# Modulation rows computed in two column halves, inside the feature projection and the preceding output projection

## The reference, cut to what matters

```python
def _layer(x, c, p):
    mod = jax.nn.silu(c) @ p['ada_w'] + p['ada_b']        # c: one row of 1024 per sequence, ada_w: 1024 x 3072
    shift, scale, gate = jnp.split(mod, 3, axis=-1)
    h = rms_norm(x, p['norm_w']) * (1 + scale[:, None, :]) + shift[:, None, :]
    z = h @ p['w_in']                                     # feature columns (1792) and token columns (1504)
    ...                                                   # RWKV-7 scan, latent attention, spatial gating
    y = jnp.concatenate([y_a, y_b, y_c], axis=-1) @ p['w_out']
    return x + gate[:, None, :] * y
```

## Time and profile before

| | |
|---|---|
| median of three runs | 5666.72 us |
| the profiled execution | 5676.56 us, its span 5674.8 us |
| TensorE busy | 5361.2 us, 94% |
| VectorE, ScalarE, GpSimd busy | 50%, 36%, 12% |
| layer 1: `modulation` | about 0 to 60 us |
| layer 1: `feature_projection` | about 60 to 582 us |
| layer 2: `modulation` | 2834 to 2893 us |
| layer 2: `feature_projection` | 2893 to about 3416 us |
| granted clock of TensorE over the span | 0.973 |

### The profile page before, as it was taken

The page is one execution under the profiler, slowest core; times in us unless marked ns, Lnnn a source line. Parts: engine busy times, 40 slices in busy tenths (PEclk is TensorE's granted clock), DMA queues, the critical chain, the costliest instruction groups (busy, mean ns, idle before and its releaser), DMA issues. The chain is left out here.

```text
span 5674.8 us, 101589 instructions
## 1 busy us (share of the span) xinstructions
PE 5361.2 (94%) x42636; PEld 2906.3 (51%) x42636; DVE 2855.3 (50%) x4296; ACT 2070.2 (36%) x3469; POOL 682.1 (12%) x1070
## 2 busy tenths in 40 slices
PE   7999999989989999989989999999899899999899
PEld 2444344477874444445434443444777744444454
DVE  1222376645545555556522223866455455555465
ACT  1121455344444444431111214553444444444311
POOL 0000000045430000001100000000444400000011
PEclk9999999999999999999989999999999999999999
DMA  6121565465542111025362215654655421110243
GB/s 247 70 91 54 182 205 188 150 157 139 140 111 64 24 24 41 11 89 177 120 239 80 80 58 179 206 186 150 156 139 136 111 68 24 24 38 15 88 173 122
DMA packets 648069, 646.54 MB, mean 114 GB/s; under 512 B 226937, under 2 KB 509049, under 8 KB 640381
## 3 DMA queue, kind: packets, MB, share of 16 engines
q1 hardware_dynamic: 647176, 638.89, 36.6%
q10 hardware_dynamic: 440, 1.15, 0.1%
HBM read 372.80 MB, written 267.13 MB: 113 GB/s over the span
## 5 line engine op out<-in xcount | busy, mean ns | idle before, releaser
L434 PE MATMUL ps<-feat_hT,w_features 128*128 128x512 f32 x2240 | 972.3, 592 | 0.0
L752 PE MATMUL ps<-w_tokens,prep_hT 128*128 128x512 f32 (+1 forms) x1920 | 825.9, 590 | 19.8 <-DMA prep_hT<-s_ht 19.8
L1629 PE MATMUL ps<-att_K,att_Q 96*128 96x512 f32 x1632 | 745.0, 599 | 33.4 <-DMA att_K<-s_qkt 23.8
L434 PEld LDWEIGHTS ps<-feat_hT,w_features 128*128 128x128 f32 x2240 | 420.5, 190 | 504.1 <-issue 501.5
L1743 DVE TENSOR_REDUCE att_mx<-ps 128x1 f32<-128x1024 f32 x384 | 470.3, 1225 | 286.5 <-PE ps L1629 286.5
L752 PEld LDWEIGHTS ps<-w_tokens,prep_hT 128*128 128x128 f32 x1920 | 365.2, 192 | 471.4 <-issue 449.1
L1636 PEld LDWEIGHTS ps<-kc,att_pr 128*128 128x128 f32 x3264 | 363.0, 141 | 432.8 <-issue 319.0
L2007 PE MATMUL ps<-w_out,fin_yT 128*128 128x512 f32 x1280 | 569.1, 598 | 2.5 <-DVE fin_yT L1965 2.5
L1636 PE MATMUL ps<-kc,att_pr 128*128 128x128 f32 x3264 | 478.9, 279 | 5.3 <-DVE att_PT L1752 2.5
L1707 ACT ACTIVATE att_PT<-ps 128x512 f32<-128x512 f32 x384 | 227.9, 594 | 691.7 <-PE ps L1636 691.7
L1629 PEld LDWEIGHTS ps<-att_K,att_Q 96*128 96x128 f32 x1632 | 297.1, 192 | 336.2 <-issue 257.2
(11 more groups left out here) (222 smaller groups left out, 7354.7 us busy)
## 6 DMA issues: line engine op xcount, KB each, us to landing
s_sc<-prep_sc SPq DMA_DIRECT2D x20, 3072.0 KB, 9.6
scan_src<-s_sc SPq DMA_DIRECT2D x80, 768.0 KB, 8.0
mod_ada<-in_ada_w SPq DMA_DIRECT2D x16, 1536.0 KB, 9.1
s_qkt<-scan_work SPq DMA_DIRECT2D x40, 576.0 KB, 4.7
fin_z<-s_zt SPq DMA_DIRECT2D x40, 576.0 KB, 5.2
s_zf<-feat_co SPq DMA_DIRECT2D x88, 256.0 KB, 2.5
s_ht<-feat_hT SPq DMA_DIRECT2D x10, 2048.0 KB, 7.8
prep_hT<-s_ht SPq DMA_DIRECT2D x40, 512.0 KB, 5.5
```

The source lines that it names most:

```text
L434: last = pe.matmul(b, wf[:, k, i * P:(i + 1) * P], hT[g % 2][:, k, :], start=(k == 0), stop=(k == KD - 1))
L752: last = pe.matmul(ps[:, tiles.bank(pieces[n]), 0:c1 - c0], hT[j % NH][:, k, :], wt[:, k, c0:c1], start=(k == 0), stop=(k == KD - 1))
L1629: pe.matmul(ps[:, c, :], Q[:, t * P:(t + 1) * P], K[:, k0:k0 + G], start=True, stop=True).then_inc(scored, 1)
```

## The change

The stage `modulation` is gone. Its work stands in two other places:

- Layer 1, in `feature_projection`: SyncE loads x(0) in four pieces, then shift and scale columns of `ada_w` in eight slices through five buffers laid over `w_tokens`, then `w_features` in five pieces, then the gate columns (4096 KB, over the same place). TensorE forms `h` 0 to 5, then the 32 products of shift and scale, the small transposes, then `h` 6 and 7.
- Layer 2, in `out_projection` of layer 1: the slices are loaded after tiles 0 to 7; the four products of a slice follow `p(n,0)` of tiles 9 to 16, the small transposes follow `p(17,0)`. Their sums stay in banks 6 and 7, so the list of banks has six.
- The gate rows of both layers: 16 products at the end of group 0 of `feature_projection`; `w_tokens` is loaded only after them.

A product of the modulation now has two column halves: the columns of one go to partitions 0 and 1 of a bank, those of the other to partitions 64 and 65. The sums of squares of group 0 wait piece by piece. The bias of shift and scale comes as columns, and `amod` has two entries and no longer five. `feature_projection` has 47 semaphores in place of 20, `out_projection` 42 in place of 30.

```diff
         kc = sb("kc", [P, K_ALL])
-        col = sb("col", [P, C_ALL])
-        amod = sb("amod", [P, NG, 2, KD])
+        cols = [sb(f"col{l}", [P, C_ALL]) for l in range(LAYERS)]
+        sg = sb("sg", [P, KD, 2])
+        amod = sb("amod", [P, 2, 2, KD])
         eps = sb("eps", [P, 4])
         ident = kc[:, K_ID:K_ID + P]
-        sems = dict(nc=nc, d=d, ps=ps, kc=kc, col=col, amod=amod, eps=eps, ident=ident)
+        sems = [dict(nc=nc, d=d, ps=ps, kc=kc, col=cols[l], amod=amod, eps=eps, ident=ident) for l in range(LAYERS)]
...
         for l in range(LAYERS):
             with nc.sbuf_tensor(f"w_tokens{l}", [P, KD, WT], F32) as wt:
                 with nc.sbuf_tensor(f"w_features{l}", [P, KD, WF], F32) as wf:
-                    modulation(l, wf, **sems)
-                    feature_projection(l, wf, wt, wt_in, **sems)
-                token_projection(l, wt, wt_in, **sems)
-            rwkv_scan(l, **sems)
...
+BANK_M = 6
+
+
+def modulation_products(pe, ps, ada, sg, k):
+
+    for b in range(2):
+        for c in range(2):
+            at = 512 * (2 * b + c)
+            last = pe.matmul(ps[64 * c:64 * c + 2, BANK_M + b, :], sg[:, k, :], ada[:, at:at + 512], start=(k == 0), stop=(k == KD - 1))
+    return last
+
+
+def modulation_turned(pe, ps, rows, ident):
+
+    for b in range(2):
+        for m in range(4):
+            for c in range(2):
+                half, at = slice(64 * c, 64 * c + 2), 2 * (4 * b + m)
+                last = pe.transpose(ps[:, BANK_M + c, at:at + 2], rows[half, 512 * b + m * P:512 * b + (m + 1) * P], ident[half, 64 * c:64 * c + 2])
+    return last
+
+
+def modulation_columns(v, ps, col, amod, summed):
+
+    made = ps[:, BANK_M:BANK_M + 2, 0:16].rearrange("p c (b m s) -> p b s c m", b=2, s=2)
+    column = lambda at: col[:, at:at + KD].rearrange("p (c m) -> p c m", c=2).unsqueeze(1).to_broadcast([P, 2, 2, 4])
+    scale, shift = (amod[:, :, n, :].rearrange("p s (c m) -> p s c m", c=2) for n in range(2))
+    v.tensor_tensor(scale, made[:, 1, :, :, :], column(C_ADAB + KD), ALU.add).then_inc(summed, 1)
+    v.wait_ge(summed, 1)
+    v.scalar_tensor_tensor(scale, scale, 1.0, column(C_NORM), ALU.add, ALU.mult).then_inc(summed, 1)
+    v.tensor_tensor(shift, made[:, 0, :, :, :], column(C_ADAB), ALU.add).then_inc(summed, 1)
+
...
+        if g == 0:
+            order.append(("gate", 0, 0))
     for u in order:
-        uses.add(u, "dve" if u[0] == "h" else "act")
+        uses.add(u, "act" if u[0] == "f" else "dve")
+
+    NA = 5
+    flat = wt[:, :, :].rearrange("p k n -> p (k n)")
+    ada = [flat[:, 2 * D * n:2 * D * (n + 1)] for n in range(NA)]
+    ada_g = flat[:, 0:KD * D].rearrange("p (k n) -> p k n", k=KD)
+    parts = [(0, 1), (1, 2), (2, 4), (4, 8), (8, NFB)]
...
-                block, x_in, zeroed, square_sums, roots, normed, filled, act_out, dve_out, edges, centre, tapped, conv, kept0, kept1, o0, o1, o2, o3, g0, g1):
+        ct = sb("ct", [P, KD, 2])
+        gb = sb("gb", [P, 512])
+        gr = sb("gr", [P, 512])
+        mrows = sb("mrows", [P, 2 * 512]) if l == 0 else None
...
                 def load_x(g):
                     if g:
                         sp.wait_ge(filled, uses.ready(("h", g - 1, KD - 1)))
-                    sp.dma_start(x[:, :, :], (d["x"] if l == 0 else d["xs"])[g * G:(g + 1) * G, :].rearrange("(j p) n -> p j n", p=P)).then_inc(x_in, 16)
+                        sp.dma_start(x[:, :, :], rows_of[g * G:(g + 1) * G, :].rearrange("(j p) n -> p j n", p=P)).then_inc(x_in, 16)
+                    else:
+                        for j in range(TPG):
+                            sp.dma_start(x[:, j, :], rows_of[j * P:(j + 1) * P, :]).then_inc(first[j], 16)
...
                 load_x(0)
-                sp.dma_start(wt[:, :, :], d["w_t"][:, l * KD:(l + 1) * KD, :]).then_inc(wt_in, 16)
+                if l == 0:
+                    for n in range(KD):
+                        if n >= NA:
+                            sp.wait_ge(used, n - NA + 1)
+                        sp.dma_start(ada[n % NA], d["ada_w"][:, n, 0:2 * D]).then_inc(part[n % NA], 16)
+                for n, (m0, m1) in enumerate(parts):
+                    sp.dma_start(wf[:, :, m0 * P:m1 * P], d["w_f"][:, l * KD:(l + 1) * KD, m0 * P:m1 * P]).then_inc(wf_in[n], 16)
+                if l == 0:
+                    sp.wait_ge(made, 1)
+                sp.dma_start(ada_g, d["ada_w"][:, l * KD:(l + 1) * KD, 2 * D:3 * D]).then_inc(ada_g_in, 16)
...
+                    if g == 0:
+                        sp.wait_ge(gate_s, 1)
+                        emptied(sp, ("gate", 0, 0))
+                        for c in range(2):
+                            sp.dma_start(d["gate"][:, 512 * c:512 * (c + 1)], gr[64 * c:64 * c + 2, :]).then_inc(gate_sent, 16)
+                        sp.wait_ge(filled, uses.ready(("gate", 0, 0)))
+                        sp.dma_start(wt[:, :, :], d["w_t"][:, l * KD:(l + 1) * KD, :]).then_inc(wt_in, 16)
+                sp.wait_ge(gate_sent, 32)
...
-                    a.wait_ge(x_in, 16 * (g + 1))
                     if g:
+                        a.wait_ge(x_in, 16 * g)
...
                     for j in range(TPG):
+                        if g == 0:
+                            a.wait_ge(first[j], 16)
...
+                if l == 0:
+                    a.dma_start(ct[:, :, :], d["c"]).then_inc(c_in, 16)
+                    for n in range(LAYERS):
+                        a.dma_start(cols[n][:, :], d["cols"][n * P:(n + 1) * P, :]).then_inc(c_in, 16)
+                    a.dma_start(kc[:, :], d["consts"]).then_inc(consts_in, 16)
+                for c in range(2):
+                    n0 = R_ADAB + 2 * D + 512 * c
+                    a.dma_start(gb[64 * c:64 * c + 2, :], d["rows"][l:l + 1, n0:n0 + 512].to_broadcast([2, 512])).then_inc(bias_in, 16)
+                if l == 0:
+                    a.wait_ge(c_in, 16 * (1 + LAYERS))
+                    a.activation(sg[:, :, :], ct[:, :, :], ACT.Silu).then_inc(silu, 1)
                 square(0)
+                if l == 0:
+                    a.wait_ge(made, 1)
+                    for b in range(2):
+                        a.activation(mrows[64:66, 512 * b:512 * (b + 1)], ps[64:66, BANK_M + b, :], ACT.Copy).then_inc(rows_s, 1)
...
+                if l == 0:
+                    v.memset(eps[:, 0:3], -0.5).then_inc(setd, 1)
+                    v.memset(eps[:, 3:4], 1.0).then_inc(setd, 1)
                 normalise(0)
+                if l == 0:
+                    v.wait_ge(c_in, 16 * (1 + LAYERS))
+                    v.wait_ge(made, 1)
+                    for b in range(2):
+                        v.tensor_copy(mrows[0:2, 512 * b:512 * (b + 1)], ps[0:2, BANK_M + b, :]).then_inc(rows_s, 1)
+                    v.wait_ge(turned, 1)
+                    modulation_columns(v, ps, col, amod, amod_s)
+                    v.wait_ge(amod_s, 3)
                 for k in range(KD):
...
+                    if g == 0:
+                        u = ("gate", 0, 0)
+                        v.wait_ge(bias_in, 32)
+                        v.wait_ge(filled, uses.ready(u))
+                        for c in range(2):
+                            rows = slice(64 * c, 64 * c + 2)
+                            v.tensor_tensor(gr[rows, :], ps[rows, uses.bank(u), :], gb[rows, :], ALU.add).then_inc(dve_out if c else gate_s, 1)
...
             @block.tensor
             def _(pe):
+                if l == 0:
+                    pe.wait_ge(consts_in, 16)
...
+                    if l == 0 and u == ("h", 0, BANK_M):
+                        pe.wait_ge(silu, 1)
+                        for n in range(KD):
+                            pe.wait_ge(part[n % NA], 16 * (n // NA + 1))
+                            last = modulation_products(pe, ps, ada[n % NA], sg, n)
+                            last.then_inc(made if n == KD - 1 else used, 1)
+                        pe.wait_ge(rows_s, 4)
+                        modulation_turned(pe, ps, mrows, ident).then_inc(turned, 1)
+                        pe.wait_ge(amod_s, 3)
...
+                    elif name == "gate":
+                        pe.wait_ge(ada_g_in, 16)
+                        for k in range(KD):
+                            for c in range(2):
+                                last = pe.matmul(b[64 * c:64 * c + 2, :], sg[:, k, :], ada_g[:, k, 512 * c:512 * (c + 1)], start=(k == 0), stop=(k == KD - 1))
                     else:
+                        for n, (m0, m1) in enumerate(parts):
+                            if g == 0 and i == m0:
+                                pe.wait_ge(wf_in[n], 16)
...
         if n + 1 < NT:
             order += [("sv", n + 1), ("ya", n + 1), ("yb", n + 1), ("yc", n + 1)]
         order += [("p", n, 1)]
-    uses = Uses()
+    uses = Uses(BANK_M)
...
+        more = l + 1 < LAYERS
+        ada = sb("ada", [P, KD, 2 * D]) if more else None
+        mrows = sb("mrows", [P, 2 * 512]) if more else None
+        FIRST = 9
...
@@ -1863,6 +1920,8 @@
```

(45 more changed lines are left out.)

26 lines of the change are left out of this document (18 added, 8 removed).

## The result

The changed kernel takes 5607.7 us (median of 4 runs, 5606.5 to 5608.5); the kernel before, beside it on the same chip, 5668.3 (5664.6 to 5676.9). The ratio is 0.9891, with an interval of 0.9874 to 0.9908: faster by 1.1%. The forecast was 5597.6, range 5584 to 5621.

What follows compares the result with a forecast made beforehand. TensorE, busy 94% of the span, was taken as the bound, with idle time at both layers' starts. Won 43.4 and 62.0, paid 36.3: 69.1 us off, taken from the runs' median, gives 5597.6 us, range 5584 to 5621.

Steps and rivals of the forecast that it cites:

- layer 1, first feature product: Start of layer 1: first feature product at 39.3 us instead of 82.7, 43.4 us won.
- x(1) of layer 1 lands: Layer 1's loads: x(1) lands at 70 to 72 us against a limit of 75, covered by 3 to 4 us.
- I take the difference off the median: Last step: the saving from an execution of 5676.6 us, 9.8 above the runs' median, is subtracted from that median, giving 5597.6.
- The sum: Whole kernel: 43.4 won in layer 1 plus 62.0 in layer 2, less 36.3 paid, gives 69.1 us off.
- the first three pieces are squared meanwhile: Layer 1's start: three pieces of x(0) are squared during loading, the last takes 1.2 us, done at 11.6.
- hidden, by 1 us: Layer 1's modulation products: the last slice lands at about 32 us, its products start at 33.2, so no wait.
- idle for 1 to 2 us: Layer 1's load queue: the sixth slice waits for a buffer until slice 0 is used (22.7), idling the queue 1 to 2 us.
- its limit: Feature stage: x(1) may land 35.7 us after the first feature product without delaying group 1; in layer 1, at 75 us.
- A: Rival: column halves do not overlap in long sequences of modulation products; saved 27.7 us, time 5639; chance 0.08.
- B: Rival: loads come late, with 1 to 2 us for a lower clock; +7, 5605, or 5616 at 0.30 MB/us; chance 0.14.
- C: Rival: six banks stall TensorE, 40 tiles taking 72 us and more; 5670 to 5690; chance 0.02.
- D: Rival: overlap starts earlier, semaphores cost nothing and x(0) lands sooner; 5588; chance 0.06.

Runs made afterwards that it cites:

- the other order: Changed kernel with a slice's four products issued as banks 0 and 1 of the first half, then of the second; 5610.3 us, ratio 0.9885.
- two slices first: Changed kernel with the products of slices 0 and 1 issued ahead of the first transposes of layer 1; 5603.5 us, ratio 0.9876.
- both improvements: Changed kernel with slices 0 and 1 multiplied before the first transposes and semaphores cleared by four engines; 5596.2 us, ratio 0.9874.
- the delay of 5.2 us: Changed kernel with 1920 KB more, unused, queued ahead of x(1) in both layers; x(1) landed 5.2 us later; 5616.3 us, ratio 0.9894.
- one column half: Changed kernel with the second column half of slices 1 to 6 written to the first's partitions, sums wrong; 5637.4 us, ratio 0.9935.

## Why the prediction was right, and what was off

The mechanism held, and most terms did. In us:

| step | foreseen | measured |
|---|---|---|
| layer 1, first feature product | 39.3 | 41.36 |
| layer 2, first feature product into the stage | 19.2 | 18.7 |
| gate rows of layer 1 | 7.1 | 7.0 (first instruction to the next of another kind) |
| a slice in the output projection | 1.96 | 2.02 |
| small transposes in the output projection | 1.4 and 0.3 | 1.5, of which 0.63 is the wait for VectorE |
| a semaphore | 0.06 | 0.063, of which 0.058 from one clear to the next |
| tile without a slice, six banks | no longer | 15.50, no longer |
| x(1) of layer 1 lands | 70 to 72 | 76.4 |
| x(1) of layer 2, after the issue of x(0) | 46 to 48 | 49.1 |

**The number** was 10.1 us too low, and the step that made most of this is the last one: "I take the difference off the median." The sum came from an execution of 5676.6 us, and 5676.6 less 69.1 is 5607.5; the changed kernel's profiled execution took 5607.75. By the profiled executions the step off the median made 9.9 us of the miss, and the sum 0.2.

That 0.2 is partly luck. The stages that the change touches (layer 1's start, output projection of layer 1 and features of layer 2, last output projection) take 1829.4 and 1828.8 us in the two profiles of the kernel before, 1761.6 and 1762.7 in those of the changed one: 66 to 68 less, so the sum was 1 to 3 too high, mostly by the start of layer 1. The other stages take 3845.4 and 3843.9 before, 3844.4 and 3845.6 after, and 3836 to 3852 in the versions that leave the semaphores alone: the scatter between executions lies there (the first token stage took 547.1 and 541.8 in two profiles of the same changed kernel).

The medians say less. On the two occasions on which both kernels ran beside each other they are 60.6 and 59.9 apart. On the two others the kernel before was slower (5676.1 and 5674.1), and on the first of these the other order, whose stages are those of the changed kernel but for a fall of the clock, was 65.8 below it. Both profiles of the kernel before are of executions of 5674 to 5677 us, so they don't show where the faster ones save time. The change is worth 60 us by the medians and 66 to 68 by the stages of the profiled executions; what the difference is stays open, and with it whether the median was a bad number to start from.

**Layer 1's start** came 2.1 us late. The prediction had "the first three pieces are squared meanwhile"; but the first sum of squares stands behind the Silu on ScalarE, and that waits for its columns until 7.97. So the four run in series and end at 12.95; the last piece has landed at 11.17, where the prediction had 10.4, so with one left to do they would have ended at 12.4. The transposes began at 17.33 and not 15.8: 0.8 us by the landing, 0.6 by the Silu, the rest in roots and scaling. The last slices cost 0.2 and 0.69 us of waiting, where I had put "hidden, by 1 us". The window 22.6 to 33 has 263 GB/s: the queue stands still, for slices 5 to 7 need buffers which only products at 22.6 and later set free. The fifth slice has landed at 24.01, the sixth is issued at 24.55 and lands at 29.36; the prediction had "idle for 1 to 2 us" here. The run with two slices first has no such wait. Its products end 4.6 us earlier, 3.4 of them by two slices that no longer stand behind the transposes and 0.9 by the waits, and the clock took back 0.6 before the first feature product. The run with both improvements has waits of 0.19 and 0.69 again, and its products end at the same time (33.10 and 33.14).

**x(1)** came 4 to 6 us later than foreseen in layer 1. About half of it has the same cause: what wasn't moved before 33 was still to be moved, and with two slices first, where the queue doesn't stand still, x(1) lands 3.3 us earlier (73.11). The other 1 to 3 us stay open. I had its limit right in kind: group 1 was ready 1.2 us before TensorE wanted it, where I foresaw 3 to 4, and the delay of 5.2 us produced a wait of 3.24 and not 5.2. In layer 2 the prediction's own numbers (17.8 MB at 0.42 MB/us, and 3) give 45.4 and not 46 to 48; it was 49.1.

**The rivals.** A (no overlap) is excluded by the 1.72 us a slice, and its price is confirmed by the run with one column half: 29.7 for six slices of eight, so about 40 for all, against the 41.4 in the rival. B (loads late) came about in small, 0.9 us of waits; its clock loss of 1 to 2 us was 1.3 to 1.7 in six of the experiments and nothing in the changed kernel. The Trainium skill (DMA: Bandwidth & Descriptors, Where 436 GB/s comes from) would have had the queue at no more than about 358 GB/s; the window 42 to 44 shows 388, so that rule didn't bind here. C (six banks) is excluded: no tile is longer than its slice. D had one thing right, 0.5 us in layer 2.

## What to carry to other kernels

A product that uses few columns of the array can be cut in two column halves that run at once: here 128x512 products with 2 columns went from 0.86 us to 0.43 us each, for 0.3 us at each entry between full-width products, and their order inside a slice made no difference. Work that is too small to be a stage of its own (58 us in each layer) belongs into stages that leave engines or time free, but then each transfer it adds stands ahead of the next group's rows, and each stage pays 0.06 us for each semaphore it clears. When a difference is worked out from one execution, compare it with the difference of two executions, and get the medians from enough runs of both kernels beside each other; here the two ways are some 7 us apart, more than the errors of all terms together.

## What the runs showed of the hardware

An issue instruction of SyncE's queue is not always short. With much in the queue (an estimate from its 23.9 us to landing and the 401 GB/s of that stretch: 9.6 MB, itself included), the timeline of that queue in the changed kernel has x(1) issued over 10.06 us; x(0) took 0.40 before:

```profile
52.49 10.06 SPq L244 DMA_DIRECT2D feat_x<-in_x  x1
```

The first store of results stood behind it, ready at 58.15 and issued at 62.60; TensorE did not wait for it. Clearing a semaphore costs differently by engine (0.058 us on SyncE, 0.084 on VectorE), so dividing them by four leaves 0.084/4 = 0.021 for each and saves 0.037, where equal engines would save 0.043. And instructions of two column halves run in pairs even when the two products of the same half are written next to each other. Last, after a gap of some 4 us with little work, the clock of TensorE fell to its lower level in six profiles and not in four others with a gap of 3.6 us.
